# The opening and the last phase of a two-block transformer kernel rearranged, and waits set per unit

## What is computed

```
m  = silu(c) @ w_mod[l] + b_mod[l]          # nine vectors of 1024 per layer, for x; mc for the context
mod_norm(x, i) = rms_norm(x, g) * (1 + m[3i+1]) + m[3i]
# block 1, per layer: FFN (swiglu, d_ff 2816), conv / pool / neighbourhood attention mixer, FFN,
# on x (256 tokens) and, but for the end of layer 1, on the context (256 tokens)
x  = x + 0.5 * m[2] * swiglu(mod_norm(x, 0))
return rms_norm(x, final_g)
# block 2, per layer: x = x + merged_attentions(rmsnorm(x)) @ w_out
u  = causal_conv3(rmsnorm(x) @ w_up) + b ;  x = x + (silu(u_a) * u_v) @ w_down
return rmsnorm(x, norm_final)
```

## Time and profile before

| what | us |
|---|---|
| runs shown, median (lowest to highest of 3) | 2761.18 (2761.11 to 2763.08) |
| the profiled execution | 2765.37 |
| its span | 2763.4 |
| TensorE busy | 2659.9 (96%) |
| VectorE busy | 1463.4 (53%) |
| ACT busy | 1122.9 (41%) |
| POOL busy | 385.7 (14%) |
| mean granted TensorE clock | 0.988 of full |
| HBM read | 397.21 MB, 144 GB/s over the span |

### The profile page before, as it was taken

The page is one execution under the profiler, slowest core; times in us unless marked ns, Lnnn a source line. Parts: engine busy times, 40 slices in busy tenths (PEclk is TensorE's granted clock), DMA queues, the critical chain, the costliest instruction groups (busy, mean ns, idle before and its releaser), DMA issues.

```text
span 2763.4 us, 44363 instructions
## 1 busy us (share of the span) xinstructions
PE 2659.9 (96%) x17192; PEld 2324.1 (84%) x17192; DVE 1463.4 (53%) x2113; ACT 1122.9 (41%) x1737; POOL 385.7 (14%) x374
## 2 busy tenths in 40 slices
PE   3999999999999999999999999989999999999998
PEld 2777879779787878777887799988999998899998
DVE  3333335565333335333346555576668777657776
ACT  2322224344222224222233454455556565565554
POOL 3100001033101011101020120120012012002211
PEclk8999999999999999999999999999999999999999
DMA  8555443214545445444323256544455654456563
GB/s 265 175 175 167 126 149 104 84 54 131 185 137 165 124 130 173 136 155 144 99 84 92 81 164 183 166 131 124 141 167 172 183 173 141 123 152 179 170 183 110
DMA packets 653900, 400.56 MB, mean 145 GB/s; under 512 B 11898, under 2 KB 614954, under 8 KB 653610
## 3 DMA queue, kind: packets, MB, share of 16 engines
q1 hardware_dynamic: 651914, 395.01, 47.2%
q0 software_dynamic: 1824, 3.29, 0.7%
HBM read 397.21 MB, written 1.05 MB: 144 GB/s over the span
## 4 chain that ended last, share of the span: by engine, by line
PE 86%; DVE 8%; ACT 3%; issue 1%; DMA 1%; POOL 0%; SPq 0%; DVEq 0%; ACTq 0%; POOLq 0%
PE psum L2173 17%; PE psum L2174 17%; PE psum L2175 17%; PE psum L2285 3%; PE psum L2287 3%; PE psum L2286 3%; DVE w_lo L1235 3%; PE psum L1952 2%; PE psum L2139 2%; PE psum L1990 2%; PE psum L2140 2%; PE psum L2141 2%; PE psum L1992 2%; PE psum L1991 2%; PE psum L2348 1%
## 5 line engine op out<-in xcount | busy, mean ns | idle before, releaser
L1235 DVE TENSOR_TENSOR w_lo<-raw,w_hi 128x1024 fp32r<-128x1024 f32 x609 | 785.8, 1290 | 673.1 <-ACT w_hi L894 671.4
L894 ACT ACTIVATE w_hi<-raw 128x1024 fp32r<-128x1024 f32 x609 | 638.7, 1053 | 417.1 <-PE psum L2175 268.1
L2173 PE MATMUL psum<-H_hi,w_hi 128*128 128x256 f32 (+1 forms) x2128 | 720.9, 339 | 13.3 <-DVE w_lo L1235 7.0
L2174 PE MATMUL psum<-H_hi,w_lo 128*128 128x256 f32 (+1 forms) x2128 | 714.9, 336 | 0.0
L2175 PE MATMUL psum<-H_lo,w_hi 128*128 128x256 f32 (+1 forms) x2128 | 714.4, 336 | 0.0
L2173 PEld LDWEIGHTS psum<-H_hi,w_hi 128*128 128x128 f32 x2128 | 404.9, 190 | 77.5 <-issue 28.9
L2175 PEld LDWEIGHTS psum<-H_lo,w_hi 128*128 128x128 f32 x2128 | 404.9, 190 | 41.8
L2174 PEld LDWEIGHTS psum<-H_hi,w_lo 128*128 128x128 f32 x2128 | 404.9, 190 | 38.9
L1840 POOL TENSOR_TENSOR G_lo<-g,G_hi 128x512 f32 (+3 forms) x132 | 141.9, 1075 | 1439.4 <-ACT G_hi L1010 1138.6
L2285 PE MATMUL psum<-H_hi,w_hi 128*128 128x256 f32 (+1 forms) x960 | 300.6, 313 | 2.4 <-ACT U L1132 2.4
L2287 PE MATMUL psum<-H_lo,w_hi 128*128 128x256 f32 (+1 forms) x960 | 285.4, 297 | 0.0
(11 more groups left out here) (246 smaller groups left out, 3954.9 us busy)
## 6 DMA issues: line engine op xcount, KB each, us to landing
raw<-ffn_w_in SPq DMA_DIRECT2D x176, 512.0 KB, 3.9
raw<-w_in SPq DMA_DIRECT2D x148, 512.0 KB, 3.9
quad_ring<-w_mod SPq DMA_DIRECT2D x66, 1024.0 KB, 6.7
raw<-w_up SPq DMA_DIRECT2D x88, 512.0 KB, 4.1
raw<-ffn_w_out SPq DMA_DIRECT2D x64, 512.0 KB, 3.7
raw<-w_out SPq DMA_DIRECT2D x32, 512.0 KB, 3.7
raw<-w_down SPq DMA_DIRECT2D x32, 512.0 KB, 3.8
raw<-ffn_w_out SPq DMA_DIRECT2D x32, 384.0 KB, 3.3
```

The costliest lines, as they stand in the source:

```text
L894: act.activation(w_hi[:, slot, :], raw[:, slot, :], ACT.Copy).then_inc(hi_done, 1)
L1235: dve.tensor_tensor(w_lo[:, slot, :], raw[:, slot, :], w_hi[:, slot, :].bitcast(F32), ALU.subtract).then_inc(lo_done, 1)
L2173: pe.matmul(o, wh, xh[:, k, 0:width], start=k == 0, stop=False)
L2174: pe.matmul(o, wl, xh[:, k, 0:width], start=False, stop=False)
```

## The change

It has four parts; the rest of the program is as it was.

1. *Opening.* Tokens are loaded in four DMAs with a semaphore each; the parameter rows after the first tile are issued by ACT. ACT squares the tokens as they lie in memory (tokens on partitions) with the accumulating form, so that POOL's adds and the ones products fall away. Transposes go by half token blocks. The quads are taken in the order 2, 3, 0, 1; the scale is applied in the product with the spread root, the shift by ACT and VectorE while they split high and low. POOL's bias and pool weight loads wait for `mod_ready`. The ring halves are loaded after the first weight tile instead of the third.
2. *Layer 1's narrow store.* Two of its evictions and the splits for units 4 and 5 move into the norm.
3. *Waits per unit.* In the four unscaled phases unit after unit runs six of eight k, waiting for its own split and bank; the statistics go before the last joint unit, the spread before k 6 and 7 of all. `conv_glu` waits for its bank only. The first two in-place multiplications of `conv_glu` move between the fourth and the fifth product of the norm.
4. *End.* ACT applies the gain after each residual tile, TensorE turns it two units later within the phase; the root (per token, which is now on partitions) is applied while the banks are emptied, by VectorE for the first 128 tokens and ACT for the others; four DMAs store the output.

```diff
@@ sync: opening
+            for tb in range(4):
+                src = (x if tb < 2 else ctx).rearrange("b (t p) d -> p (b t) d", p=P)
+                sp.dma_start(tokens_in[:, tb:tb + 1, :], src[:, tb % 2:tb % 2 + 1, :]).then_inc(s_tok[tb], 16)
+            for j in range(3):
                 for half in range(2):
+                    sp.dma_start(quad_first[j][:, 4 * half:4 * half + 4, :], quad_weights(FIRST_QUADS[j], 0, half)) \
+                      .then_inc(quad_first_in[j][half], 16)
...
-                    if u == 2 and ph.start == 0 and first:
+                    if u == 0 and ph.start == 0 and first:
@@ scalar
+        for p0, tile, n, ap in row_pieces:
+            if tile > 0:
+                act.dma_start(rows_in[p0:p0 + n, tile, :], ap).then_inc(s_rows, 16)
...
+            for tb in range(4):
+                act.wait_ge(s_tok[tb], 16)
+                at_least(act, tok_sq, tb)
+                act.activation(sq[:, :, :].rearrange("p a t -> p (a t)"), tokens_in[:, tb, :], ACT.Square,
+                               accum_out=row_sum[:, tb:tb + 1]).then_inc(stat_done if tb == 3 else tok_sq, 1)
...
+                if "ends" in ph.more:
+                    square(ph.more["norm_next"], f, src)
+                    act.activation(T2[:, f, :], src, ACT.Copy, scale=vec("norm_final", f)).then_inc(final_gain, 1)
+                    return
...
                 for k in range(KD):
                     high_half(nm, 1, k)
+                    if k in (1, 4) and nm["next"].width == S:
+                        split_ahead(nm["next"], 1 if k == 1 else 2, 0)
@@ vector: opening
+        def first_norm(nm):
+            quad_to_rows(0)
+            quad_sums(0, FIRST_QUADS[0])
+            quad_to_rows(1)
+            quad_sums(1, FIRST_QUADS[1])
+            first_scale()
+            dve.wait_ge(rstd_spread, 1)
+            for k in range(KD):
+                if k == 4:
+                    quad_to_rows(2)
+                    quad_sums(2, FIRST_QUADS[2])
+                for s in range(2):
+                    cols = slice(s * S, s * S + S)
+                    ins = dve.scalar_tensor_tensor(T1[:, k, cols], X[:, k, cols], modv[:, 0, 1, k, s:s + 1], STAT[:, cols],
+                                                   ALU.mult, ALU.mult)
+                ins.then_inc(n_mul, 1)
+            quad_to_rows(3)
+            first_split(0)
+            quad_sums(3, FIRST_QUADS[3])
...
+            ins.then_inc(mod_ready, 1)
+            first_split(1)
+            dve.wait_ge(mod_ready, 1)
+            for k in range(KD):
+                dve.wait_ge(h_hi_done, k + 1)
...
+                if k == 2:
+                    first_split(2)
@@ vector: norms
+                    if k in (2, 5) and nm["next"].width == S:
+                        u = 0 if k == 2 else 1
+                        scaled_store(nm["next"], u)
+                        split_ahead(nm["next"], u + 1, 0)
...
+                for fh in range(2):
+                    dve.wait_ge(final_t, 2)
+                    dve.tensor_scalar(tokens_out[:, 0, fh * 512:fh * 512 + 512], bank[4 + fh][:, :], rstd_tok[:, 0:1], None,
+                                      ALU.mult).then_inc(final_copy, 1)
...
                 for k in range(KD):
+                    if k == 4 and nm["next"].kind == "conv_glu":
+                        dve.wait_ge(rs_copied, nm["x0"] // KD + 1)
+                        spread_raw(nm["next"], 0)
+                        spread_raw(nm["next"], 1)
@@ gpsimd
-        pool_w_load(0)
-        bias_load(0)
...
+            if kind == "first":
+                pool.wait_ge(mod_ready, 1)
+                pool_w_load(0)
+                bias_load(0)
@@ tensor
+        def raw_units(ph, n, nm):
...
+            for v in range(n):
+                pe.wait_ge(lo_done, ph.start + v + 1)
+                pe.wait_ge(acc_free, ph.start + v - 3)
+                if v == n - 1:
+                    pe_stats(nm)
+                for k in range(kk - 2):
+                    if v == 0:
+                        pe.wait_ge(xg_lo, nm["x0"] + k + 1)
+                    raw_product(v, k)
+            pe_spread(nm)
+            for k in range(kk - 2, kk):
+                pe.wait_ge(xg_lo, nm["x0"] + k + 1)
+                for v in range(n):
+                    ins = raw_product(v, k)
...
+                    if "ends" in ph.more and 4 * i + u >= 2:
+                        final_turn(4 * i + u - 2)
...
-                    if first or ph.more.get("pair"):
+                    if first or ph.kind == "glu":
...
+        def final_turn(f):
...
+            pe.wait_ge(final_gain, f + 1)
+            for tb in range(2):
+                ins = pe.transpose(bank[4 + 2 * tb + f // 4][:, f % 4 * P:f % 4 * P + P], T2[:, f, tb * P:tb * P + P], ident)
+            if f >= KD - 2:
+                ins.then_inc(final_t, 1)
```

More of the change, by code:

```diff
@@ L277, in build_program @@
     s_rows = sem("s_rows")
-    s_tok = sem("s_tok")
+    s_tok = [sem(f"s_tok{tb}") for tb in range(4)]
+    tok_sq = sem("tok_sq")
     s_bias = sem("s_bias")
@@ L442, in norm @@
             affines[0] += KD
-        if kind != "final":
+        if kind == "final":
+            [ph for what, ph in plan if what == "gemm"][-1].more["ends"] = nm
+        else:
             splits[0] += KD
@@ L453, in norm @@
         plan.append(("norm_stats", nm))
-        if more.get("ahead"):
+        if kind == "first":
             plan.append(("quads", None))
-            plan.append(("mod_read", (0, "scale")))
         plan.append(("norm", nm))
@@ L499, in build_program @@
             plan.append(("tokens", None))
-            norm("mod", width=512, seg=0, ahead=True)
+            norm("first", width=512, seg=0)
             ffn(512, ffn_w_in[layer, 0], ffn_w_out[layer, 0], 0, True,
@@ L994, in step @@
                     t = ph.start + u + ph.stride * i
-                    if not (first and u == 0 and ("raw_first" in ph.more or "halved" in ph.more)):
+                    ahead = 0 if not first else 3 if "halved" in ph.more and width == S else \
+                        1 if "raw_first" in ph.more or "halved" in ph.more else 0
+                    if u >= ahead:
                         split_ahead(ph, u, i)
@@ L1074, in act_norm_stats @@
                 return
+            if nm["kind"] == "first":
+                act.wait_ge(tok_sq, 3)
+                act.wait_ge(stat_done, 1)
+                act.activation(rstd_tok[:, 0:4], row_sum[:, 0:4], ACT.Sqrt, scale=1.0 / D, bias=eps[:, 0:1]).then_inc(rms_done, 1)
+                return
             if "next" in nm:
@@ L1402, in step @@
                 if raw and k == "conv_glu":
-                    for u in range(3):
-                        spread_raw(ph, u)
+                    spread_raw(ph, 2)
                 for u in range(n_units):
                     t = ph.start + u + ph.stride * i
-                    if not (first and u == 0 and (raw or "halved" in ph.more)):
+                    narrow = first and "halved" in ph.more and width == S
+                    if u >= (3 if narrow else 1 if first and (raw or "halved" in ph.more) else 0):
                         split_ahead(ph, u, i)
@@ L1452, in step @@
                             raw_low(ph, f - 1)
+                    elif k == "store" and first and ph.more.get("scale_first"):
+                        if not (narrow and u < 2):
+                            scaled_store(ph, u)
                     elif k == "store":
@@ L1458, in step @@
                             dve.tensor_tensor(dst[:, f, 0:width], bank[b][:, 0:width], spread_copy[:, :], ALU.mult).then_inc(acc_free, 1)
-                        elif first and ph.more.get("scale_first"):
-                            dve.tensor_scalar(dst[:, f, 0:width], bank[b][:, 0:width], SCALE, None, ALU.mult).then_inc(acc_free, 1)
                         else:
```

206 lines of the change are left out of this document (122 added, 84 removed).

## The result

| | before | changed |
|---|---|---|
| median, first set of runs | 2761.91 us (4 runs, 2761.11 to 2763.08) | 2720.96 us (4 runs, 2717.07 to 2721.93) |
| median, last set of runs | 2762.78 us (9 runs, 2761.30 to 2767.20) | 2720.36 us (5 runs, 2720.13 to 2721.33) |
| ratio, 95% interval | 1 | 0.9849 [0.9832, 0.9866]; last set 0.9846 [0.9833, 0.986] |
| the profiled execution shown | 2765.37 us, span 2763.4 | 2717.07 us, span 2715.3 |

The change makes the kernel 1.5% faster: 41.0 us between the medians of the first set, 42.4 in the last. The prediction was 2716.5 us with a range of 2704 to 2734; the median came out 4.5 us above it. Three further single runs of the kernel before, made beside the experiments, took 2761.63, 2767.75 and 2768.36 us, so that its time varies by some 7 us.

The account below looks back on a forecast made before the run. TensorE carried 86% of the chain that ended last, so its gaps had to shrink, though it waits for others at both ends. Gains 22.4 + 8.1 + 3.0 + 6.6 + 2.0 + 2.6 = 44.7 gave 2716.5 us, range 2704 to 2734.

Parts of the forecast that it names:

- The opening: Start to first FFN product: VectorE's chain decides, product at 44 us instead of 66.4, gain 22.4; 41 to 49 possible.
- Rival (a): Opening bound by data: at 303 GB/s 11.4 MB land at 42, first product at 48, total 2721 us; chance 0.15.
- First block-2 projection: Units no longer all wait for the third split; spread at 1814.2 instead of 1822.30, gain 8.1 us, 4 if clock falls.
- Second projection: Second block-2 projection: the 2.79 us stall and 1.5 us of half clock go; gain 3.0 us (1.5 to 4).
- `conv_glu`: Fifth and sixth units stop waiting for several freed banks; 3.3 us in each of two layers, 6.6 (2 to 7.5).
- Narrow store: Layer 1: fifth unit's split moves before the norm's end, start 1468.4 instead of 1470.28; gain 2.0 us (0 to 5).
- The end: Last residual phase and tail: tail 6.7 us instead of 15.7, last product 6.4 later; gain 2.6 (-2 to +6).
- The sum: Whole kernel: six gains add to 44.7 us, subtracted from the runs' median 2761.18 for 2716.5 us.
- (b): Around block 2 waits only change their name, VectorE stays the bound; 15 of 17.7 us come back, 2732; chance 0.1.
- (c): Opening: tokens and quads stay serial because row transposes stand ahead; only 11 us gained, 2728; chance 0.08.
- (d): Behind `mod_ready` the moved gather starves the weights, TensorE stands and falls to half clock; slower, 2770 at 65 us; chance 0.02.
- (e): Whole kernel: no change, from several shares of all the other rivals at once; chance 0.01.

Follow-up runs that it names:

- nine profiles: Profiles with the changed opening: the first one, two unedited repeats, six with edits elsewhere in the kernel; first product between 43.68 and 46.48 us.
- the repeats: The changed kernel run again twice, nothing edited: 2721.21 us in a single run, then a median of 2720.36 us over five.
- the version with four edits: Changed kernel plus tokens turned before parameter rows, two column-group copies on ScalarE, final turns one unit later, table load later: median 2710.87 us, ratio 0.9807.
- the second repeat: The changed kernel unedited, timed five times beside the version with four later edits: median 2720.36 us (2720.13 to 2721.33).
- the later turns: Changed kernel with each finished output tile of the last residual phase turned three units after its own, not two: 2714.49 us.

## Why the prediction was right, point by point

**The opening**: 22.4 forecast, 22.7 in the profiled pair, 22.35 against the median of nine profiles. The chain held within 0.9 us at each step: forecast 14.1, 20.5, 23.5, 30.9, 34.7, 36.4, 39.6 and 42.1, in the first profile 15.0 (end of the row tiles), 21.4, 23.6, 30.6, 34.4, 36.4, 39.5 and 41.6. Two steps were off, and they cancel. The first: "ACT starts issuing 1.6 us earlier than SP did, so 12.0". The rows released TensorE at 12.83 to 13.66 in the nine profiles, at the median at 13.01. By the Trainium skill (DMA: Bandwidth & Descriptors, Issuing engines are not separate DMA queues) issuing from another engine saves only the sequencer's time, and the prediction read from it 13.6, as before. All nine lie nearer to that than to my 12.0, though 0.6 us of the 1.6 were gained; and the run with the early gather shows that other traffic moves the landing by 6.4. The second: reciprocal, diagonals and spread took 2.3 us instead of 3, since the spread ran at 1.10 us where 2.07 had been taken from the row of before. That the sum fits is luck of the clock: in the repeats, where the spread took 2.04 and 2.05 again, the product came at 45.7 and 46.5. Rival (a), data, is out as to what decides: "the last quad lands near 33 us" came out as 33.4, 2.7 us before it was wanted at 36.07. The "6 us of slack" of the data were less than that.

**First block-2 projection**: 8.1 forecast, 7.4 to 7.6 measured, both by the pair and by putting the old order back. The mechanism stands. The forecast put the spread at 1814.2 instead of 1822.30; on the time scale of before (the changed kernel is 29.1 us ahead at the mark before this stretch) it came at 1814.9. TensorE waits 0.79 + 1.29 us in the first unit for VectorE, which the estimate had allowed for by "unit 0 does six k by 1808", and 0.19 before the spread; the 0.7 us is the whole miss.

**Second projection**: 3.0 forecast, 3.4 in the pair and 3.56 by the experiment. **`conv_glu`**: 6.6 forecast, 6.9 in the pair (3.5 and 3.4) and 7.3 by the experiment; 3.76 us less what the early multiplications hand back fits in size. That the 0.61 us wait that stayed is their 0.4 is not shown, as no run puts them back. **Narrow store**: 2.0 forecast, 1.9 measured.

**The end**: 2.6 forecast, 1.3 in the pair, 2.1 with the repeats against the old ending. The stall of 3.4 was 3.17, its half clock of 1.8 was 2.6 in the first profile and 1.5 in the repeats, the tail of 6.7 was 7.2. By the Trainium skill (TensorE: Matmul & The Clock Gate, Part 4: PE-mode transpose) the full clock doesn't engage for transposes, and the prediction had priced that at up to 8 us of half clock. The runs show no such thing: the later pairs of turns took 0.38 us inside a stream at full clock, and with the first pair's wait shortened there is no half clock in that phase up to the last product. The token transposes of before, from which the prediction read this, stood alone on TensorE for 10.4 us ahead of them and 6.9 behind.

**The sum**: 44.7 forecast. The terms as measured in the pair, with the opening's median and the repeats' ending, are 22.4 + 7.4 + 3.4 + 6.9 + 1.95 + 2.1 = 44.2. What failed is the last line, which subtracted the sum from the median of the runs: "the median of the runs shown lies 4.2 lower". The gain between the medians is 41 to 42.4 us. The price list came from one execution that took 2765.37, which is 3.5 us above the median of the first set of runs and 2.6 above that of the last, and its opening had the slow clock (2.07 for the spread, 2.70 for the first column group), so part of what the sum removes may not have been in the median. That the 2 to 3 us between the sum and the medians lie there fits the spread of the changed kernel, but was not shown: of the kernel before there is only one trace.

Rivals (b), (c), (d) and (e) are out by the runs named above; of (c) it holds that the row transposes stand ahead of the tokens', but moving them was worth 2.9 us, not 11. For (d): with the gather issued from 44.2 us, beside the first products, TensorE is busy without a gap from 50 to 100 us, at full clock, while the DMA engines move 154 to 237 GB/s (in windows of 10 and 20 us): in the changed kernel the weights were never short there. In the version with four edits, which starts 4 us earlier, they were once, for 1.1 us.

## What to carry to other kernels

A chain of waits written down step by step, each with a duration from a row of its own, forecast an opening to 0.4 us, but with two misses that cancelled: a landing taken from an issue time, and a duration taken from a row at half clock. When work is moved into a phase, look at what the engines do ahead of its first piece: here an early table load of 1.3 us cost 3 us, because TensorE stood for it and then ran slow. Read what a stall costs as idle time plus the half clock behind it, and take a sum of small gains against a median only after looking at how the one profiled execution stood to it.

## What the runs showed of the hardware that was not expected

The same kernel with the same stalls gets different spells of half clock, and that is most of its spread of 5 us. The granted clock in stretches (columns: stretch, its length, busy time and instructions of TensorE, its weight loads, VectorE, ScalarE and POOL, then the granted clock, the DMA share and GB/s), first profile of the changed kernel, then the second repeat:

```profile
40.00:50.00 10.00, 6.98 (x25) 5.48 (x26) 9.16 (x21) 8.35 (x18) 7.81 (x13) 0.83 1.09 355
1549.00:1562.00 13.00, 11.38 (x99) 10.62 (x98) 5.21 (x9) 5.06 (x7) 0.00 (x0) 1.00 0.28 82
2690.00:2698.00 8.00, 6.93 (x37) 6.96 (x38) 4.42 (x6) 4.23 (x8) 2.29 (x2) 0.57 0.20 50
```

```profile
40.00:50.00 10.00, 5.85 (x26) 3.87 (x15) 9.16 (x20) 6.33 (x15) 5.79 (x10) 0.67 0.94 309
1549.00:1562.00 13.00, 9.71 (x69) 8.98 (x70) 6.17 (x10) 4.39 (x7) 0.00 (x0) 0.87 0.14 42
```

Behind the wait of 3.19 us near 1550 the clock stays at 2.4 GHz in the one (1.00) and falls to 1.2 GHz for a while in the other (0.87). In two more profiles, those of the later turns and of the old ending, it stays up behind that wait and falls 8 us later, behind one of 1.62 us. The wait of 2.5 us near 1445 is the same in twelve profiles; a spell of 1.2 to 1.5 us follows it in three and none in nine. In the version with four edits the first FFN products run at full clock at once after 2.58 us of idle time (0.39 us a product), where all others lose 1.2 to 2.4 us to half clock (counted from the products' durations). In the profile with the old narrow store the same first wait is also 2.58 us, and the products behind it start at half clock. What decides it is open: the length of the stall alone does not. A difference of 2 or 3 us between single runs of this kernel is thus no evidence for an edit; the length between two marks is.
